# Sorted experts: rows gathered by token lists, weights in pairs, results scattered by token

## What is computed

```python
h = jax.nn.silu(jnp.einsum('td,edf->tef', t, w_gate)) * jnp.einsum('td,edf->tef', t, w_up)
y = jnp.einsum('tef,efd->td', h * combine[..., None].astype(h.dtype), w_down)
```

## Time and profile before

| | us |
|---|---|
| median of 3 runs | 4072.62 |
| the profiled execution | 4070.53 |
| its span | 4068.8 |
| experts: end of `place_experts` to the first normalizing step (2748 to 3032 of the span) | 284 |

### The profile page before, as it was taken

How to read it: one execution, slowest core, us unless ns; L and a number is a source line. 1 busy time by engine, 2 the same in 40 slices (tenths; PEclk the granted TensorE clock), 3 DMA queues, 4 the chain that set the end, 5 groups by cost and what they waited for, 6 DMA issues and landing times. The chain is left out here.

```text
span 4068.8 us, 43607 instructions
## 1 busy us (share of the span) xinstructions
PE 3582.0 (88%) x15846; PEld 2435.1 (60%) x15846; DVE 2836.6 (70%) x5091; ACT 846.0 (21%) x1666; POOL 896.9 (22%) x856
## 2 busy tenths in 40 slices
PE   8999998778778777777999998986988999999998
PEld 6778775223223222222667776865766787877876
DVE  7553678778878877865754466766877558757775
ACT  2111022111111111110121135415852312411000
POOL 2010004444434444443000021204540000100000
PEclk9999999999999999999999998997999999999999
DMA  7322228999999999998334432129962233223221
GB/s 290 137 93 94 96 104 323 420 423 423 423 423 423 423 422 419 410 419 368 113 120 146 146 109 88 51 96 381 416 260 83 79 94 99 83 94 101 96 88 70
DMA packets 206417, 910.08 MB, mean 224 GB/s; under 512 B 20958, under 2 KB 25966, under 8 KB 126738
## 3 DMA queue, kind: packets, MB, share of 16 engines
q0 software_dynamic: 93040, 665.54, 40.0%
q1 hardware_dynamic: 108272, 233.47, 17.1%
q10 hardware_dynamic: 4900, 8.42, 0.6%
HBM read 878.45 MB, written 40.97 MB: 226 GB/s over the span
## 5 line engine op out<-in xcount | busy, mean ns | idle before, releaser
L176 PE MATMUL psum<-ring_high,h_features 128*128 128x512 f32 x1128 | 459.9, 408 | 31.3 <-PEq L48 14.5
L130 DVE CAST ring_high<-ring_raw 128x2048 fp32r<-128x2048 f32 (+2 forms) x163 | 187.9, 1153 | 417.3 <-PE psum L178 340.4
L178 PE MATMUL psum<-ring_high,h_features 128*128 128x512 f32 x1128 | 446.6, 396 | 0.0
L177 PE MATMUL psum<-ring_low,h_features 128*128 128x512 f32 x1128 | 446.2, 396 | 0.0
L1769 PE MATMUL psum<-slots_ring,evacuation_tmp 128*128 128x512 f32 x672 | 333.3, 619 | 91.4 <-DVE evacuation_tmp L1863 91.4
L176 PE MATMUL psum<-h_features,ring_high 128*128 128x512 f32 (+3 forms) x888 | 349.5, 394 | 11.2 <-DVE ring_low L132 4.5
L132 DVE TENSOR_TENSOR ring_low<-ring_raw,ring_high 128x2048 fp32r<-128x2048 f32 (+2 forms) x163 | 349.5, 2144 | 12.6 <-issue 0.4
L177 PE MATMUL psum<-h_features,ring_high 128*128 128x512 f32 (+3 forms) x888 | 346.7, 390 | 0.0
L178 PE MATMUL psum<-h_features,ring_low 128*128 128x512 f32 (+3 forms) x888 | 346.7, 390 | 0.0
L1985 ACT ACTIVATE weight<-score 128x1 f32<-128x1 f32 x512 | 103.6, 203 | 1123.5 <-DVE score L1870 1123.3
L1769 PE MATMUL psum<-slots_features,evacuation_tmp 128*128 128x512 f32 x504 | 251.9, 624 | 63.7 <-DVE evacuation_tmp L1863 63.5
(11 more groups left out here) (679 smaller groups left out, 7020.2 us busy)
## 6 DMA issues: line engine op xcount, KB each, us to landing
ring_raw<-in_w_in SPq DMA_DIRECT2D x94, 1024.0 KB, 5.3
ring_raw<-in_w_up_pairs SPq DMA_DIRECT2D x20, 1024.0 KB, 5.0
ada_ring<-in_w_ada POOLq DMA_DIRECT2D x16, 1024.0 KB, 5.6
ring_raw<-in_w_out SPq DMA_DIRECT2D x12, 1024.0 KB, 5.1
moe_entries<-in_const_zero_rows POOLq DMA_DIRECT2D x23, 512.0 KB, 4.8
row_room<-moe_entries SPq DMA_DIRECT2D x23, 512.0 KB, 11.1
moe_results<-rows_out SPq DMA_DIRECT2D x23, 512.0 KB, 7.6
ring_raw<-in_w_down SPq DMA_DIRECT2D x10, 1024.0 KB, 4.9
```

Of the source, the lines that this page charges most:

```text
L130: nc.vector.tensor_copy(high, whole)
L176: nc.tensor.matmul(out, a[0], b[0], start=start, stop=False)
L177: nc.tensor.matmul(out, a[0], b[1], start=False, stop=False)
L178: return nc.tensor.matmul(out, a[1], b[0], start=False, stop=stop)
```

## The change

The rows' way is turned round. In `place_experts` SP stores the 512 tokens plainly to `moe_tokens`. At the head of `moe` VectorE (`spot_rows`), eight small matmuls on TensorE and VectorE again (`list_tokens`) make for every row of every tile the number of its token, or 4096 where the row is unfilled. GpSimd then gathers the rows of each tile from `moe_tokens` with these numbers, and scatters each tile's results with them to the place 2 x token + choice of `moe_results`; numbers out of bounds move nothing. The results come back by four plain loads of 1 MB on SP. Nothing is cleared in DRAM; the two row places are set to zero once by GpSimd. Pieces 0 and 1 of a tile come in one gather of 2 MB (`pair`) and piece 2 in another (`single`), two places each. There are 2 row places where there were 4. The four vectors are loaded after the outputs of tiles 14 to 17.

```diff
@@ -2329,14 +2329,11 @@
         pool.wait_ge(on.rows_kept, 16)
         for h, spread in enumerate((on.spread0, on.spread1)):
             pool.dma_start(row[:, h, :], core.gate_rows[h, :].partition_broadcast(P)).then_inc(spread, 16)
-        for s in range(ROW_TILES):
-            pool.wait_ge(on.updated, s + 1)
-            if s == 2 * LEVELS - 2:
-                pool.wait_ge(on.decayed, 2)
-                pool.wait_ge(on.masked, 2 * LEVELS)
-                for h, spread in enumerate((on.spread0, on.spread1)):
-                    pool.dma_start(row[:, h, :], core.gate_rows[2 + h, :].partition_broadcast(P)).then_inc(spread, 16)
-            pool.dma_start(core.moe_entries[s * P:(s + 1) * P, :], d["const_zero_rows"]).then_inc(core.entries_cleared, 16)
+        pool.wait_ge(on.updated, 2 * LEVELS - 1)
+        pool.wait_ge(on.decayed, 2)
+        pool.wait_ge(on.masked, 2 * LEVELS)
+        for h, spread in enumerate((on.spread0, on.spread1)):
+            pool.dma_start(row[:, h, :], core.gate_rows[2 + h, :].partition_broadcast(P)).then_inc(spread, 16)
...
         @block.sync
         def _(sp):
             sp.dma_start(bias[:], d["router_bias_2"].partition_broadcast(P)).then_inc(loaded, 16)
             sp.dma_start(lower_first[:], d["const_before"].partition_broadcast(P)).then_inc(loaded, 16)
+            for t in range(NT):
+                sp.dma_start(core.moe_tokens[t * P:(t + 1) * P, :], core.x[:, t, :]).then_inc(core.tokens_stored, 16)
             load_ahead(core, sp, core.splits + 2)
 
...
-            nc.gpsimd.iota(piece_steps[:], pattern=[[1, PIECES]], base=-P * PIECES, channel_multiplier=PIECES,
+            nc.gpsimd.iota(piece_steps[:], pattern=[[1, 1]], base=-P, channel_multiplier=1,
                            allow_small_or_imprecise_dtypes=True)
             nc.gpsimd.iota(kinds[:], pattern=[[1, 2]], base=1, channel_multiplier=0, allow_small_or_imprecise_dtypes=True).then_inc(ready, 1)
+            nc.gpsimd.iota(row_steps, pattern=[[1, P]], base=0, channel_multiplier=0, allow_small_or_imprecise_dtypes=True)
+            nc.gpsimd.iota(token_codes, pattern=[[2 * P, NT], [1, 2]], base=1, channel_multiplier=2, allow_small_or_imprecise_dtypes=True)
+            pool.wait_ge(core.products, QUARTERS * (first + 1))
+            nc.gpsimd.memset(row_room, 0.0).then_inc(cleared, 1)
+            pool.wait_ge(cleared, 1)
 
...
-RAW_PIECES, CUT_PIECES, ROW_PLACES = 5, 4, 4
+RAW_PIECES, CUT_PIECES, ROW_PLACES, RAW_PLACES = 5, 4, 2, 2
+NO_TOKEN = 4096.0
...
+        row_room = over(nc, core.hT_whole, "row_room", [P, 2 * ROW_PLACES, D])
+        rows_in = row_room[:, 0:ROW_PLACES, :]
+        last_single = row_room[:, ROW_PLACES:2 * ROW_PLACES, :].rearrange("p a n -> p (a n)")
...
+            pair_place = lambda s: raw[:, 2 * (s % RAW_PLACES):2 * (s % RAW_PLACES) + 2, :].rearrange("p a n -> p (a n)")
+            single_place = lambda s: (raw[:, 2 * RAW_PLACES, :], last_single)[s % RAW_PLACES]
+            raw_piece = lambda s, piece: single_place(s) if piece == 2 else raw[:, 2 * (s % RAW_PLACES) + piece, :]
...
             @block.gpsimd
             def _(pool):
-                pool.wait_ge(core.entries_cleared, 16 * ROW_TILES)
-                for t in range(NT):
-                    for which in range(2):
-                        nc.gpsimd.indirect_dma_start(out=entries, out_offset=bass.IndirectOffsetOnAxis(ap=rows_of[:, t, which:which + 1], axis=0),
-                                                     in_=core.x[:, t, :], in_offset=None).then_inc(sorted_rows, 16)
+                def pair(s):
+                    if s >= RAW_PLACES:
+                        pool.wait_ge(cut_high, turn[s - RAW_PLACES, 1] + 1)
+                        pool.wait_ge(cut_low, turn[s - RAW_PLACES, 1] + 1)
+                    nc.gpsimd.indirect_dma_start(out=pair_place(s), out_offset=None, in_=d["moe_pairs_2"],
+                                                 in_offset=bass.IndirectOffsetOnAxis(ap=pieces_of[:, s:s + 1], axis=0)).then_inc(pair_in[s % RAW_PLACES], 16)
+
+                def single(s):
+                    if s >= RAW_PLACES:
+                        pool.wait_ge(cut_high, turn[s - RAW_PLACES, 2] + 1)
+                        pool.wait_ge(cut_low, turn[s - RAW_PLACES, 2] + 1)
+                    nc.gpsimd.indirect_dma_start(out=single_place(s), out_offset=None, in_=d["moe_singles_2"],
+                                                 in_offset=bass.IndirectOffsetOnAxis(ap=pieces_of[:, s:s + 1], axis=0)).then_inc(single_in[s % RAW_PLACES], 16)
+
+                def enter(s):
+                    if s >= ROW_PLACES:
+                        pool.wait_ge(row_turned, s - ROW_PLACES + 1)
+                    nc.gpsimd.indirect_dma_start(out=rows_in[:, s % ROW_PLACES, :], out_offset=None, in_=core.moe_tokens,
+                                                 in_offset=bass.IndirectOffsetOnAxis(ap=tokens_of[:, s:s + 1], axis=0),
+                                                 bounds_check=SEQ - 1, oob_is_err=False).then_inc(row_in[s % ROW_PLACES], 16)
+
+                pool.wait_ge(core.tokens_stored, 16 * NT)
                 pool.wait_ge(pieced, 1)
-                for n, (s, piece) in enumerate(taken):
-                    if n >= RAW_PIECES:
-                        pool.wait_ge(cut_high, n - RAW_PIECES + 1)
-                        pool.wait_ge(cut_low, n - RAW_PIECES + 1)
-                    nc.gpsimd.indirect_dma_start(out=raw[:, n % RAW_PIECES, :], out_offset=None, in_=d["moe_rows_2"],
-                                                 in_offset=bass.IndirectOffsetOnAxis(ap=pieces_of[:, s, piece:piece + 1], axis=0),
-                                                 ).then_inc(piece_in[n % RAW_PIECES], 16)
-                pool.wait_ge(cut_high, len(taken))
-                pool.wait_ge(cut_low, len(taken))
-                for b in range(2):
-                    pool.wait_ge(stored[b], 16 * ((ROW_TILES + 1 - b) // 2))
-                for t in range(NT):
-                    for which in range(2):
-                        nc.gpsimd.indirect_dma_start(out=returned[:, 2 * t + which, :], out_offset=None, in_=results,
-                                                     in_offset=bass.IndirectOffsetOnAxis(ap=rows_of[:, t, which:which + 1], axis=0),
-                                                     ).then_inc(back[2 * t + which], 16)
+                pair(0)
+                pool.wait_ge(read, 1)
+                enter(0)
+                enter(1)
+                pair(1)
+                for s in range(2):
+                    single(s)
+                def leave(s):
+                    pool.wait_ge(evacuated, 2 * (s + 1))
+                    nc.gpsimd.indirect_dma_start(out=results, out_offset=bass.IndirectOffsetOnAxis(ap=results_of[:, s:s + 1], axis=0),
+                                                 in_=rows_out[:, s % 2, :], in_offset=None,
+                                                 bounds_check=2 * SEQ - 1, oob_is_err=False).then_inc(stored[s % 2], 16)
+
+                for s in range(2, ROW_TILES):
+                    pair(s)
+                    enter(s)
+                    if s >= 3:
+                        single(s - 1)
+                    if s >= 4:
+                        leave(s - 4)
+                single(ROW_TILES - 1)
+                for s in range(ROW_TILES - 4, ROW_TILES):
+                    leave(s)
...
             @block.sync
             def _(sp):
-                def enter(s):
-                    if s >= ROW_PLACES:
-                        sp.wait_ge(row_turned, s - ROW_PLACES + 1)
-                    sp.dma_start(rows_in[:, s % ROW_PLACES, :], tile(entries, s)).then_inc(row_in[s % ROW_PLACES], 16)
-
-                def leave(s):
-                    sp.wait_ge(evacuated, 2 * (s + 1))
-                    sp.dma_start(tile(results, s), rows_out[:, s % 2, :]).then_inc(stored[s % 2], 16)
-
                 load_ahead(core, sp, 2 * values + 2)
-                sp.wait_ge(sorted_rows, 16 * 2 * NT)
-                for s in range(ROW_PLACES):
-                    enter(s)
-                for buf, vec in ((core.row_a[:], d["ln2_g_2"][0]), (core.row_b[:], d["ln2_b_2"][0]), (in_gain, d["in_ln_g_3"]), (in_shift, d["in_ln_b_3"])):
+                vectors = [(core.row_a[:], d["ln2_g_2"][0]), (core.row_b[:], d["ln2_b_2"][0]), (in_gain, d["in_ln_g_3"]), (in_shift, d["in_ln_b_3"])]
+                sp.wait_ge(read, 1)
+                for n, (buf, vec) in enumerate(vectors):
+                    sp.wait_ge(evacuated, 2 * (ROW_TILES - 2 * len(vectors) + n))
                     sp.dma_start(buf, vec.partition_broadcast(P)).then_inc(vectors_loaded, 16)
-                for s in range(ROW_TILES):
-                    if s + ROW_PLACES < ROW_TILES:
-                        enter(s + ROW_PLACES)
-                    if s:
-                        leave(s - 1)
-                leave(ROW_TILES - 1)
-                for b in range(2 * NT):
```

(57 more changed lines are left out.)

45 lines of the change are left out of this document (27 added, 18 removed).

## The result

The changed kernel takes 4105.24 us (median of 4 runs, 4096.71 to 4106.85) against 4072.11 us (4 runs, 4071.34 to 4074.38). The ratio is 1.0076, 95% interval 1.0059 to 1.0094: slower by 0.8%, where 4058.6 was predicted. The profiled execution has a span of 4102.4 us against 4068.8, at a granted clock of 0.971 against 0.975; the difference of the spans, 33.6 us, is what I take apart.

What follows compares the result with a forecast made beforehand. DMA engines bound the loop at 10.0 us a tile, TensorE close behind at 9.5. Savings of 8.9 us (6.4 from the head) and 5.1 (tail), 14.0 from 4070.53, give 4056.5, plus 2.1 for the median 4058.6; range 4046 to 4075.

Steps and rivals of the forecast that it cites:

- The recurrence: Expert loop: T(s+2) is at least T(s) + 19.57 us + w, the filled rows' transfer; period 9.8 to 10.4 us.
- Start of the pair: GpSimd in the loop: the pair starts at T(s) + 7.45, after the cut ends at T(s) + 7.3.
- a rival with a chance of 0.15: Loop: pair starts under VectorE's next subtraction and issues 2 us longer, 11 x 2 = 22 us, 4080.6 us; chance 0.15.
- Issue of the pair: GpSimd in the loop: issuing the pair's gather takes 0.94 us, the undisturbed value.
- From the issue's end to the rows: Loop: 2.2 us latency, 5.0 us pair data, then w, the tile's filled rows x 4 KB / 419 GB/s.
- From the rows to the next products: TensorE in the loop: 0.05 us, then 3.97 us from the row transposes to the next tile's start.
- The head: Start of experts: first transposes at 2762, tile 2's rows cost 3.8 us wait, 6.4 us saved; bounds 5 to 9.
- The tail: Results' return: plain loads bring the first normalizing step to 3026.9 from 3032.04, 5.1 us saved; bounds 3 to 6.5.
- The clearing: `delta_scan`, ahead of the experts: removing the clearing stores of 0.5 MB each gives 0 to 2 us.
- half the DMA engines: Loop: if a row's place decides its engine, filled rows cost 6.6 instead of 3.7 us, 4061.5 us; chance 0.15.
- TensorE's bound: Loop: with shorter gather latency TensorE's 9.53 us a tile holds, 4048.6 us; chance 0.17.
- The two smallest rivals: Loop: 16 KB rows or bounds test add 0.94 us a pair, 4068.9, chance 0.12; unfilled rows move, 4067.4, chance 0.06.

Runs made afterwards that it cites:

- filler work: Changed kernel plus 24 identity transposes on TensorE ahead of the row transposes of every second tile: 4091.90 us, ratio 1.0057.
- the cut moved: Changed kernel with the third piece's cut of tile s put behind the row halves of tile s+2: 4090.22 us, ratio 1.0038.
- rows first: Changed kernel with GpSimd issuing a tile's row gather ahead of its weight pair, not behind: 4054.66 us, ratio 0.9954.
- spreading: A tile's filled rows placed alternately in both halves of the partitions: 4103.20 us on the changed kernel, 4047.22 us with its row gather ahead of the pair.
- the fastest version: Changed kernel with row gather ahead of pair, third cut behind row halves, rows over both partition halves: 4042.30 us, again 4040.06 us (ratio 0.9924).

## Why the prediction was wrong

The recurrence was right: T(s+2) hangs on T(s) through the cut, the pair, the rows behind it, and TensorE's wait for `moe_tokens` is the new bound. Its terms were not. For the two tiles from 2852.08 to 2877.14:

- Cut of the second piece done at T + 7.34; the prediction had 7.3. Right.
- **Start of the pair**: 0.15 us later by the prediction, 0.78 measured. This is the step that failed: the prediction gave no row for how long GpSimd takes to start after such a wait, and took next to nothing. It is small by itself, but "it just misses the next subtraction at T(s) + 8.1" hung on it: 7.34 + 0.78 = 8.12, and the subtraction starts at 7.97. I had named this as a rival with a chance of 0.15. The kernel before could have told it. A weight gather that had waited for a subtraction's end, 2785.79, starts 0.77 us behind it, under the next subtraction, and takes 2.25:

```profile
2783.46 2.33 DVE L3526 TENSOR_TENSOR third_cut<-raw,third_cut 128x2048 fp32r<-128x2048 f32 x1
2785.72 2.28 DVE L3526 TENSOR_TENSOR last_cut<-raw,last_cut 128x2048 fp32r<-128x2048 f32 x1
...
2786.56 2.25 POOL L3321 DMA_INDIRECT raw<-in_moe_rows,pieces_of  x1 [2.16 <-DVE third_cut L3526]
```

- **Issue of the pair**: 0.94 by the prediction, called the undisturbed one; 2.99 measured, 2.05 more. Of the 64 weight gathers of before behind the first five 35 took over 2 us, so 0.94 was the rarer case and not the default. What a start under the subtraction costs was predicted well (2 us a pair, 22 us); its removal gave 14. What the traces show of such starts stands in the last section.
- **From the issue's end to the rows**: 8.66 measured against 7.16 + 0.52 for that tile's 53 rows, 0.98 more.
- **From the rows to the next products**: 5.29 against 4.02. The clock fell in the wait of 3.71 us. I had priced this fall at the head and left it out in the loop, because I expected idling of 0.4 us; run with filler work, it is worth 9.8 us of the stage.

0.63 + 2.05 + 0.98 + 1.27 = 4.9 us over the predicted 20.1. From T(1) to T(21) it took 253.2 us where 199.4 was predicted; ten such steps are 49 of the 53.8 us between them. The terms feed each other through the clock: in the changed kernel TensorE's 11 waits of 2.24 to 5.29 us between 2770 and 3030 each go with a stretch at 0.50, while with the cut moved its 10 waits of 1.18 to 2.00 us between 2848 and 2949 have none. That is why the size went beyond the rival's 4080.6, which had the long issue alone.

- The head: the first row transposes came 17.9 us before those of the earlier trace rows, 8.1 of it gained ahead of the experts, so 9.8 by the head itself (10.65 predicted). The rows of tile 2 made TensorE wait 5.29 us where 3.8 was predicted. 3.9 us saved, not 6.4.
- The tail: 5.3 us saved, 5.1 predicted; idle 0.70 us ahead of `merge` at full clock, 1 us predicted. Right.
- The vectors' loads, `place_experts`' stores and zeros: nothing visible, as taken.
- The clearing: 0 to 2 us predicted, 6.5 measured in one stretch, in every profile alike; the 8.1 between the profiles and the 10.5 by putting it back hold differences that have nothing to do with it. I looked at who waits for the stores and not at what runs beside them.
- Rivals: half the DMA engines does not decide here; with rows first spreading goes with 2 to 6 us less of stage, which is near the scatter. That a row's place decides its DMA engine, from which the rival had 6.6 us instead of 3.7, was supposed and no run shows it: the rows land in 8.5 us spread and 8.4 not spread. TensorE's bound was reached only in the order that the change did not have, and there in stretches.
- The two smallest rivals fall away. Rows of 16 KB and the bounds test take no issue time of their own (0.93 to 0.96 and 1.01 us), and unfilled rows don't move: the stage has 2048 packets of 4 KB on GpSimd's queue, 1024 entries gathered and 1024 scattered.

## What to carry to other kernels

When a transfer is put behind another on GpSimd, write down what the first one waits for and what VectorE does in the microsecond after that: here a start 0.6 us later decided 2 us. Issue the transfer that TensorE waits for next ahead of the one that is needed two tiles later, even where it is small; here that one line was worth 50 us. And a wait in which the granted clock falls, as in the 3.71 us here, is to be priced with the slow work behind it. Last, compare the stage that a change touches and not only whole times: two profiles of one kernel reached this stage 8.9 us apart.

## What the runs showed of the hardware

- Who starts first decides whether an indirect DMA on GpSimd is held up. In the 13 profiles, from 2780 to 3000 us, 482 of them began 0.045 us or more behind the start of a VectorE subtraction with both operands in SBUF and before its end: all ended 0.80 to 0.91 us behind the subtraction's end and took 1.18 to 3.14 us. 61 began within its first 0.045 us and took 0.94 to 1.00; in 167 it began during the issue, and they took 0.93 to 1.02. 80 began under a subtraction with an operand in PSUM whose end plus 0.8 us would have made them longer than 1.1 us; they took 0.93 to 1.02. Two more, in two of the runs with the cut moved, began under VectorE's scaling of `x_tokens` (L3648, one operand, in SBUF) and took 2.57. Moving the subtraction took the slow issues of the pair away (0.93 to 0.96 us).
- GpSimd starts a DMA 0.77 or 0.78 us behind the end of the subtraction that it waited for (12 of 18 pairs in the changed kernel, 18 of 19 with the cut moved), against 0.30 between two issues.
- The DMA engines move fewer bytes at a full share than in the kernel before: 419 GB/s at 1.01 there, 374 at 0.98 in the fastest version, 344 at 0.93 with rows first, 353 at 0.94 with the layout and row size of before. Neither pairing nor the spreading explains it; the plain row loads and stores of before may, but no run tests it. What the traces show is a tail: the median 8 KB packet of weights takes 309 ns before and after, but from 2850 to 2950 us 1.8% of them take over 400 ns before and 5.7 to 12.6% in the other kernels. The cause stays open; with it 9.5 us a tile fills the engines though there is less to move.
- Beside bulk stores of 0.5 MB TensorE stopped twice for 1.9 to 2.6 us in a run of tiny matmuls, without any semaphore between them, each time until 1.4 us behind the end of a 16 KB packet of the instruction queue that started 7.2 to 7.6 us behind the one ahead of it.
